# Five of eight quads per MLP pair in the seven-product form, with wider turns and a new row order of the weight tiles

## The reference

```python
x = x + merged @ w_out[l]
h2 = rmsnorm(x, norm2_g[l])
x = x + jnp.square(jax.nn.relu(h2 @ w_mlp_in[l])) @ w_mlp_out[l]
```

## Time and profile before

| | us |
|---|---|
| median of 3 runs | 2818.17 (2817.73 to 2818.86) |
| the profiled execution | 2816.88 |
| its span, first to last instruction | 2815.1 |
| PE busy | 2803.1 |
| DVE busy | 2159.4 |
| ACT busy | 1465.2 |
| mean granted clock of TensorE | 0.999 of full speed |
| DMA | 596.55 MB, mean 212 GB/s |

### The profile page before, as it was taken

How to read it: one execution, slowest core, us unless ns; L and a number is a source line. 1 busy time by engine, 2 the same in 40 slices (tenths; PEclk the granted TensorE clock), 3 DMA queues, 4 the chain that set the end, 5 groups by cost and what they waited for, 6 DMA issues and landing times.

```text
span 2815.1 us, 33882 instructions
## 1 busy us (share of the span) xinstructions
PE 2803.1 (100%) x13174; PEld 2314.5 (82%) x13174; DVE 2159.4 (77%) x2445; ACT 1465.2 (52%) x1626; POOL 2.3 (0%) x7
## 2 busy tenths in 40 slices
PE   9999999999999999999999999999999999999998
PEld 7888878888888888888888888888888888888887
DVE  7697855556779888788877678877677888887886
ACT  6644446544456555555546444444455555555554
POOL 0000000000000000000000000000000000000000
PEclk9999999999999999999999999999999999999999
DMA  9576756666866666666777766667676766666674
GB/s 318 161 222 198 205 161 207 198 196 197 255 210 217 216 210 208 212 218 204 218 228 226 222 198 215 202 205 224 202 217 214 222 218 204 216 210 208 212 233 169
DMA packets 361824, 596.55 MB, mean 212 GB/s; under 512 B 22208, under 2 KB 95552, under 8 KB 361024
## 3 DMA queue, kind: packets, MB, share of 16 engines
q1 hardware_dynamic: 361232, 594.06, 67.6%
q10 hardware_dynamic: 432, 0.32, 0.0%
HBM read 556.81 MB, written 2.10 MB: 199 GB/s over the span
## 4 chain that ended last, share of the span: by engine, by line
PE 97%; DVE 2%; issue 1%; ACT 0%; DMA 0%; SPq 0%; DVEq 0%; ACTq 0%
PE ACC L775 76%; PE TB L781 14%; PE ACC L781 5%; DVE WL L1515 1%; DVE HT L1987 0%; PE TB L895 0%; DMA RAW<-in_w_in_dram 0%; ACT WH L1046 0%; PE TB L928 0%; PE TB L931 0%; PE TB L960 0%; PE TB L937 0%; PE TB L949 0%; DVE ZCb L1962 0%; PE TB L1000 0%
## 5 line engine op out<-in xcount | busy, mean ns | idle before, releaser
L1046 ACT ACTIVATE WH<-RAW 128x1024 fp32r<-128x1024 f32 (+1 forms) x1023 | 1046.9, 1032 | 1083.0 <-PE ACC L775 745.8
L1515 DVE TENSOR_TENSOR WL<-RAW,WH 128x1024 fp32r<-128x1024 f32 (+1 forms) x1023 | 1194.3, 1185 | 388.0 <-ACT WH L1046 385.9
L775 PE MATMUL ACC<-WH,XTH 128*128 128x512 f32 (+1 forms) x1692 | 658.5, 389 | 0.6 <-DVE XTL L2008 0.3
L775 PE MATMUL ACC<-WL,XTH 128*128 128x512 f32 (+1 forms) x1692 | 655.2, 387 | 0.0
L775 PE MATMUL ACC<-WH,XTL 128*128 128x512 f32 (+1 forms) x1692 | 655.1, 387 | 0.0
L775 PEld LDWEIGHTS ACC<-WH,XTH 128*128 128x128 f32 x1692 | 317.8, 188 | 67.7 <-DVE XTL L2008 1.2
L775 PEld LDWEIGHTS ACC<-WH,XTL 128*128 128x128 f32 x1692 | 317.7, 188 | 65.1
L775 PEld LDWEIGHTS ACC<-WL,XTH 128*128 128x128 f32 x1692 | 317.8, 188 | 64.0
L775 PE MATMUL ACC<-WH,YAH 128*128 128x512 f32 x864 | 336.2, 389 | 0.0
L775 PE MATMUL ACC<-WL,YAH 128*128 128x512 f32 x864 | 336.1, 389 | 0.0
L775 PE MATMUL ACC<-WH,YAL 128*128 128x512 f32 x864 | 336.1, 389 | 0.0
(11 more groups left out here) (335 smaller groups left out, 2821.2 us busy)
## 6 DMA issues: line engine op xcount, KB each, us to landing
RAW<-in_w_in_dram SPq DMA_DIRECT2D x255, 512.0 KB, 4.3
RAW<-in_w_mlp_in_dram SPq DMA_DIRECT2D x128, 512.0 KB, 4.5
RAW<-in_w_mlp_out_dram SPq DMA_DIRECT2D x128, 512.0 KB, 4.5
RAW<-in_w_up_dram SPq DMA_DIRECT2D x128, 512.0 KB, 4.3
RAW<-in_w_down_dram SPq DMA_DIRECT2D x128, 512.0 KB, 4.4
RAW<-in_w_gate_dram SPq DMA_DIRECT2D x96, 512.0 KB, 4.4
YT<-HT SPq DMA_DIRECT2D x208, 128.0 KB, 2.8
RAW<-in_w_branch_dram SPq DMA_DIRECT2D x48, 512.0 KB, 4.3
```

What stands on the lines that cost most here:

```text
L775: ins = e.matmul(ACC[:, 2 * (b % 2) + half, 0:n], p[:, k, xs], q[:, t, 0:n], start=(k == 0 and m == 0), stop=(k == nk - 1 and m == 2))
L1046: e.activation(WH[u % NSPL][:, ts, 0:n], RAW[u % NRAW][:, ts, 0:n], ACT.Copy).then_inc(hi, 1)
L1515: e.tensor_tensor(l, r, h, ALU.subtract).then_inc(lo, 1)
```

## The change

- `SEVEN_I` goes from (0, 2, 4, 6) to (0, 2, 3, 5, 6). Quads 2 and 3 now stand side by side, and 5 and 6. Indices, semaphore counts and the arrays of sums grow from four to five per pair; the sums of activations that no longer fit where they were lie in new tiles (`G3`, `TXF`).
- The parts of the weight sums go in turn to three places (two in `TS`, one new tile `TX`), by pairs of two: pair `k` of quad `q` takes place `(2q + k) % 3`. Its first pair waits for the quad before the last one, its second for the last one. Where two such quads are side by side (`CLOSE`), the second pair is split one unit later, on both engines.
- `YT` is no tile of its own any more: it is a view of `HB`, out of which the columns were turned. So whoever writes `HB` next (the first step of `product1_out`, of `product_sums`, and the plain blocks' `Relu`) waits for the end of the split, where it waited for the turn.
- The turns read columns that lie side by side: a row of 512 is taken as (k g t j), in its own order, where it was taken as (k j g), every fourth column. The channels so land in another order on the partitions, and the rows of the weight tiles that multiply them (`TURNED`) are loaded in that order, four vectors as well.
- The split of a turned pair comes 7 units behind the turn and no longer 9.

```diff
-    SEVEN_I = (0, 2, 4, 6)
+    SEVEN_I = (0, 2, 3, 5, 6)
...
+    CLOSE = [u for u in SEVEN_END if u - 2 in SEVEN_END]
...
-    YT["1"] = [sb(f"YT{i}1", [P, 8, P], F32, m1) for i in range(2)]
+    YT["1"] = [h[:, :, :].rearrange("p a (t n) -> p (a t) n", t=4) for h in HB["1"]]
...
+    def t_pair(tag, q, k, part):
+
+        r = (2 * q + k) % 3
+        return TX[tag][:, 2 * part:2 * part + 2, :] if r == 2 else TS[part][:, 2 * r:2 * r + 2, :]
...
-                turn_at(("h" + tag, j, b), end + 3 + 2 * b, 9)
+                turn_at(("h" + tag, j, b), end + 3 + 2 * b, 7)
...
+            rows = w[2 * i * P:(2 * i + 2) * P, c0:c0 + n]
+            rows = rows.rearrange("(g t j) n -> j (g t) n", g=4, t=2) if NAMES[b][0] in TURNED else rows.rearrange("(t p) n -> p t n", p=P)
...
-                if SEVEN.get(u + AHEAD, (0, 0))[1]:
-                    weight_sums_low(u + AHEAD)
+                if u + AHEAD - 1 in CLOSE:
+                    weight_sums_low(u + AHEAD - 1, 1)
+                if u + AHEAD in SEVEN_END:
+                    weight_sums_low(u + AHEAD, 0)
+                    if u + AHEAD not in CLOSE:
+                        weight_sums_low(u + AHEAD, 1)
...
-                    ins = e.transpose(HT[tag][q][:, :, half, :].rearrange("p g (k i) -> p k g i", k=4),
-                                      src[:, half, :].rearrange("p (k j g) -> p k g j", k=4, g=4))
+                    ins = e.transpose(HT[tag][q][:, :, half, :].rearrange("p g (k t i) -> p k g t i", k=2, t=2),
+                                      src[:, half, :].rearrange("p (k g t j) -> p k g t j", k=2, g=4, t=2))
...
-                e.tensor_tensor(sx[:, S_A], AX[:, :, 0, 0, :], r0.to_broadcast([P, 4, P]), ALU.mult).then_inc(xs, 1)
+            e.tensor_tensor(sx[S_A], AX[:, :, 0, 0, :], r0.to_broadcast([P, 5, P]), ALU.mult).then_inc(xs, 1)
...
+            e.tensor_tensor(G3[1][:, :, :], sx[S_3], G3[0][:, :, :], ALU.subtract).then_inc(xs_lo, 1)
```

More of the change, by code:

```diff
@@ L221, in build @@
     ST = sb("ST", [P, 160])
+    forms = ExitStack()
+    G3 = [sb(f"G3{n}", [P, 4, P], F32R, forms) for n in "HL"]
+    forms.close()
     GBP = sb("GBP", [P, 2, 512])
@@ L399, in build @@
     YA0 = {("at_o", 0): 0, ("at_o", 1): 2}
+    TURNED = ("wo1", "h1", "o1", "za", "zb", "zc", "g2a", "g2b", "g2c", "wo2", "h2", "o2")
     TURNS = []
@@ L803, in pair_unit @@
             q = SEVEN[u][0]
-            new, end = q % 4 == 0, q % 4 == 3
+            new, end = q % 5 == 0, q % 5 == 4
             def sums(f):
-                return [y[:, f, q % 4, :] for y in SXR] if f != S_4 else [y[:, q % 4, :] for y in S4R[tag]]
+                return [x_form(tag, f, q % 5, part) for part in range(2)]
             def weight_sums(f):
-                return [y[:, f, :] for y in TS]
+                return [t_pair(tag, q, f // 2, part)[:, f % 2, :] for part in range(2)]
             if m == 0:
@@ L1046, in cut, with sums_high @@
             e.activation(WH[u % NSPL][:, ts, 0:n], RAW[u % NRAW][:, ts, 0:n], ACT.Copy).then_inc(hi, 1)
[L1048 to L1055, removed]
+        def sums_high(u, k):
+            q, tag = SEVEN[u][0], NAMES[units[u][0]][0][1]
+            if q >= 2 - k:
+                e.wait_ge(mm, SEVEN_END[q - 2 + k] + 1)
+            e.wait_ge(t_sum, 4 * q + 2 * k + 2)
+            e.activation(t_pair(tag, q, k, 0), TR[tag][:, 2 * k:2 * k + 2, :], ACT.Copy).then_inc(t_hi, 1)
         def stream(u, front):
@@ L1529, in weight_sums, with weight_sums_low @@
             e.tensor_tensor(tr[:, T4, :], b21, tr[:, T2, :], ALU.subtract).then_inc(t_sum, 1)
[L1531 to L1538, removed]
+        def weight_sums_low(u, k):
+            q, tag = SEVEN[u][0], NAMES[units[u][0]][0][1]
+            if q >= 2 - k:
+                e.wait_ge(mm, SEVEN_END[q - 2 + k] + 1)
+            e.wait_ge(t_hi, 2 * q + k + 1)
+            e.tensor_tensor(t_pair(tag, q, k, 1), TR[tag][:, 2 * k:2 * k + 2, :], t_pair(tag, q, k, 0), ALU.subtract).then_inc(t_lo, 1)
         def stream(u, front):
@@ L2043, in x_sums @@
             e.wait_ge(rsb, int(tag))
[L2044 removed]
+            e.wait_ge(xs, m + 5)
             r0, r1, t0 = (TB[0][:, k * P:k * P + P].unsqueeze(1) for k in range(3))
[L2046 to L2050 removed]
@@ L2350, in layouts @@
     r["cst"], r["pmat"] = consts()
-    r["vecs"] = np.concatenate([v[n].reshape(-1, P) for n in VECS]).T
+    turned = ("norm2_g", "g_mix_2", "g_mlp_2", "final_g")
+    r["vecs"] = np.concatenate([v[n].reshape(-1, 4, 2, 32).transpose(0, 2, 3, 1).reshape(-1, P) if n in turned else v[n].reshape(-1, P)
+                                for n in VECS]).T
     r["x_t"] = v["x"][0].T
```

105 lines of the change are left out of this document (63 added, 42 removed).

## The result

| | before | after |
|---|---|---|
| median of the runs, us | 2817.95 (2817.33 to 2818.86) | 2833.99 (2832.85 to 2835.30) |
| ratio | | 1.0057, interval 1.0044 to 1.0070 |
| the profiled execution | 2816.88 | 2834.30 |
| its span | 2815.1 | 2832.5 |

A forecast was written before the change was run, and what follows sets the result against it. PE, busy 2803.1 of 2815.1 us, bounds the kernel, with DVE full in places. -9.5 - 2.3 - 1.0 + 9.8 + 8.8 = +5.8 gave 2822.7, median 2824.0, then 2822.5 after halving the stall price; range 2811 to 2832.

The forecast's parts named there:

- the landing of quad 5's second tile: Wait of DVE ahead of quad 5's sums for a weight tile: 0.27 us per later pair, 0.5 per first pair.
- wo2's start: At the start of wo2, faster turns shorten PE's wait for turned columns: 1.0 us gained, bounds 0 and 1.5.
- The matmuls removed: Five seven-product quads for four save one product in each of 14 pairs: 9.5 us of PE.
- the residual's stall: In pairs two to seven, PE's 0.19 us stall on the residual goes, 12 times: 2.3 us gained.
- Pairs two to seven: Last low part of quad 6 0.40 us late, plus stall price and tile: 0.82 lost per pair, 9.8 in twelve.
- the row order: Weight tiles with rows 64 apart on neighbouring partitions land unchanged at 4.5 us; bounds 0.5 less and 1 more.
- softest term: The 0.15 us added to each stall beyond its lateness, some 3 us in all; half was taken off.
- The first pairs: First pair of each MLP: stalls of 5.4 us in place of 1.0, 4.4 more each, 8.8 in all.
- Costed at nothing: Copies' waits for the split, the third place's wait and wider x sums are hidden or fall in idle time: 0 us.
- The queue keeps up: Rival: DVE's queue stalls nothing in pairs two to seven (2813.5 us, chance 0.18), or in first pairs too (2805.4, 0.13).
- Slow landings: Rival: new row order adds 1 us to a tile, late at quad 5 in 14 pairs: 2836.5 us, chance 0.10.
- Turns no faster: Rival: the write side sets the transposes' 1079 ns, so the turns gain nothing: 2825 us, chance 0.08.

The follow-up runs named there:

- e_first: The changed kernel with seven-product quads only at 0, 2, 5 and 6 in each MLP's first pair, other pairs keeping five: 2826.14 us, ratio 1.0031.
- e_rows: The changed kernel with every weight tile loaded in the plain row order again, so products mix up channels: 2831.12 us, ratio 1.0045.
- e_turn: The changed kernel with turns, row order of tiles and vectors as before the change: 2834.41 us, ratio 1.0056.
- e_four: The changed kernel with four seven-product quads per pair again (0, 2, 4, 6), activation sums still made for five: 2812.95 us, ratio 0.9981.
- e_t3: The changed kernel without one of the four weight sums (T3) in each seven-product quad, one product left wrong: 2813.84 us, ratio 0.9984.

## Why the prediction was wrong, step by step

The mechanism was right in the main: which stalls would go, which would come, where, and who would release them. The sum was too small by 11.6 us (17.4 for 5.8 in the profiled executions). The step that failed is the term for the landing of quad 5's second tile: 0.27 us in a later pair and 0.5 in a first one were forecast, 0.68 and 1.58 were measured on average, which makes 4.9 and 2.2, together 7.1 of the 11.6. The rest is DVE's steps in the later pairs, which were taken a little too short (2.4), tiles of other quads that were late (1.4), and 1.0 at the kernel's start, less 0.3 that wo2's start gained beyond its term.

**The matmuls removed, the residual's stall, wo2.** Right. 42 fewer; the residual at 0.40 as walked, and its 12 stalls gone; PE issued matmuls without a gap at wo2's start (50 in 11.00 us from 2050, of all sizes, where the earlier trace rows had 44), a gain of 1.3 for 1.0.

**Pairs two to seven: 0.82 a pair forecast, 1.49 measured by the stalls of the table, 1.6 from start to start.** The prediction made it of 0.40 of lateness, 0.15 for one stall and 0.27 for the tile. The last low part came at 33.49 on average where 32.50 was forecast without the tile. Measured:
- The landing ahead of quad 5's sums is 0.68 on average over the twelve pairs (0.22 to 1.72) and not 0.27. That tile took 4.95 us to land on average, with 4.42 of room. In the kernel before the like places had 4.57 in 4.51 at quad 4 and 4.87 in 4.72 at quad 6; the 0.27 came from all 28 of them, first pairs too, and at ten of these places DVE had just idled 0.09 to 0.33 us for ScalarE, which gave the tile time. Part of it was the row order, which was costed at nothing: the issue takes 0.23 longer. One trace says little of that part, since landings vary: in the new order the mean wait is 0.68 here and 0.51 in e_first, in the plain one 0.41 in e_rows and 0.38 in e_turn. So the row order has 0.1 to 0.3 of the 0.41 that were missing, and the rest is there without it.
- DVE's steps are 0.2 longer over the pair (0.14 of it up to quad 5 in the pair shown), so the lateness is 0.6 and not 0.40.
- Tiles of quad 2 and quad 6, costed at nothing, came late in three of the twelve pairs: 0.1 on average.
- The price of a stall, 0.16 with the 0.05 until PE starts, was right in size, and it was right to count it once, although a pair has three stalls or more.

0.60, 0.68, 0.10 and 0.16 make 1.54. Halving the "softest term" at the end, which took 1.5 off, went the wrong way: the full 0.15 was right.

**The first pairs: 5.4 each forecast, 6.5 measured.** The four stalls around quad 3 were forecast at 4.3 together and were 2.49, 0.36, 0.44 and 0.89 in the first MLP, that is 4.2. At quad 6 2.1 came for 1.07: the tile was 1.54 late and not 0.5, since it took 5.6 us to land; that two moves of the turn stand before it was rightly seen and held it up by 0.3. In the second MLP the half clock took the place of three of these stalls and added nothing.

**Costed at nothing.** The new waits for the splits and for the third place of the sums, and the wider x sums: no wait of any size on them in the list, so right. The row order: wrong, as told. The kernel's start: 1.0 us, unexplained. The Trainium skill, "DMA: Bandwidth & Descriptors", section "Latency and other measured facts", has copies between tensors in HBM whose partitions step by large powers of two lose rate; by its figures that would have made up to 0.7 us of a tile, an estimate. At the step of 2 MB, in the MLP's first matrix, the landing went from 4.5 to 4.6, and e_rows has 4.4. In its second matrix, where a row is 8 KB and the step 512 KB, it went from 4.5 to 4.9, and e_rows has 4.4. So tiles in the new order did land 0.2 to 0.5 later, 0.23 of which is the longer issue, but the larger step has the smaller part: the page's order does not show on these loads.

**The rivals.** "The queue keeps up" fell in both forms: e_four and e_t3 show that DVE's load is what stalls PE. "Slow landings" had a part of the truth in its place (quad 5) and its sign, with 0.2 where it asked 1 us (e_rows against the changed kernel, medians of the first matrix). "Turns no faster" fell (688 ns).

## What to carry to other kernels

Before an engine at the bound is relieved by work on another, walk that other engine through one whole stage, and ask whether it still comes to rest somewhere in it: with four quads DVE rests 0.3 to 1.0 us before the last one, with five it doesn't, and from there every late tile and every step that is a little longer is added to the time one for one. Find the one point of the stage where the slower engine hands over last, and count there, once: stalls of the faster engine ahead of it, even at half clock, are contained in it. A mean wait taken from a stage with some rest (0.3, longest 1.2) was too low for the stage without (0.68, longest 1.72). And try the parts of a bundled change one by one: here all parts but the named one gain 5 us, and that kernel, at 2812.95, is the best of all that ran.

## What the runs showed of the hardware

- SP takes 368 ns to issue a tile of 256 rows of 2 KB when a partition gets rows p and p + 128, and 602 when rows are taken in four groups and pairs; the bytes are the same, and the tile lands 0.2 us later in the MLP's first matrix (4.4 and 4.6) and 0.5 in its second (4.4 and 4.9).
- A stall of 2.3 us of PE was followed in one place by some 3 us at a granted clock of 0.52, and in another, as long, by none. e_rows and e_turn have the dip in the second MLP too.
- A sum of 128x512 f32 takes 1800 ns on GpSimd and 692 on DVE, and a DVE sum beside it takes 1662 in the median.
- After a stall of over 0.1 us PE's next matmul starts 0.34 behind the first and not 0.227 (all such stalls in the pairs of the changed kernel).
